# RWKV-7 recurrence without identity products, its first level on VectorE, head sums and spreads in two array groups

## The reference

```python
kk = heads(k * k_k)
kk = kk / jnp.maximum(jnp.sqrt(jnp.sum(kk * kk, axis=-1, keepdims=True)), 1e-12)
def step(S, inp):
    r_t, w_t, k_t, v_t, kk_t, a_t = inp
    sa = jnp.einsum('bhvk,bhk->bhv', S, -kk_t)
    S = (S * w_t[:, :, None, :] + sa[..., None] * (kk_t * a_t)[:, :, None, :]
         + v_t[..., None] * k_t[:, :, None, :])
    return S, jnp.einsum('bhvk,bhk->bhv', S, r_t)
# mean and variance of y over each head, then gn_w, gn_b, and
y = y + jnp.sum(r_h * k_h * r_k, axis=-1, keepdims=True) * v_h
```

## Time and profile before

| | |
|---|---|
| profiled execution, its own time | 3829.3 us |
| its span | 3827.5 us |
| mean granted TensorE clock | 0.912 |
| PE busy, whole span | 3199.8 us, 84% |
| DVE, ACT, POOL busy | 42%, 28%, 16% |
| first to last L1105 (start of a step on PE) | 1041.0 to 1969.0 us |

### The profile page before, as it was taken

One profiled execution on the slowest core, in us unless ns is written; L12 is line 12 of the kernel. 1 busy time (PEld: TensorE's weight loads), 2 busy tenths in 40 slices (PEclk: granted clock), 3 DMA queues, 4 the chain that ended last, 5 costly groups with the idle time before them and its releaser, 6 DMA issues. The chain is left out here.

```text
span 3827.5 us, 80050 instructions
## 1 busy us (share of the span) xinstructions
PE 3199.8 (84%) x35142; PEld 2529.9 (66%) x35142; DVE 1604.6 (42%) x2556; ACT 1069.8 (28%) x1930; POOL 613.2 (16%) x405
## 2 busy tenths in 40 slices
PE   3799999987588888888884984999899979992199
PEld 1687888852277777777773862888677877771077
DVE  4433333434355555555543115222277107774421
ACT  2222222212344444434342013110122115461110
POOL 0222222125221222122210000000000000342200
PEclk7899999999798999989896987999899989996599
DMA  4212222111521212222203331111122234233433
GB/s 147 77 59 80 72 69 77 58 44 77 175 69 47 74 49 72 58 64 59 62 25 116 115 126 55 39 33 34 32 66 72 73 105 138 75 96 124 131 99 110
DMA packets 287269, 301.64 MB, mean 79 GB/s; under 512 B 11807, under 2 KB 221855, under 8 KB 285296
## 3 DMA queue, kind: packets, MB, share of 16 engines
q1 hardware_dynamic: 255392, 217.64, 18.7%
q10 hardware_dynamic: 28512, 71.33, 4.8%
q0 software_dynamic: 3056, 8.05, 0.9%
HBM read 187.41 MB, written 114.25 MB: 79 GB/s over the span
## 5 line engine op out<-in xcount | busy, mean ns | idle before, releaser
L414 PE MATMUL pj_ps<-pj_x_hi,pj_w_hi 128*128 128x512 f32 x1024 | 402.1, 393 | 68.4 <-DVE pj_x_lo L369 60.1
L414 PE MATMUL pj_ps<-pj_x_lo,pj_w_hi 128*128 128x512 f32 x1024 | 400.8, 391 | 0.0
L414 PE MATMUL pj_ps<-pj_x_hi,pj_w_lo 128*128 128x512 f32 x1024 | 400.7, 391 | 0.0
L414 PEld LDWEIGHTS pj_ps<-pj_x_hi,pj_w_hi 128*128 128x128 f32 x1024 | 193.6, 189 | 112.4 <-issue 61.9
L348 POOL TENSOR_TENSOR pj_x<-h 128x512 f32<-128x512 f32 x128 | 168.0, 1313 | 575.4 <-DVE pj_x_lo L369 512.7
L369 DVE TENSOR_TENSOR pj_x_lo<-pj_x,pj_x_hi 128x512 fp32r<-128x512 f32 x128 | 89.2, 697 | 356.7 <-ACT pj_x_hi L424 356.7
L1483 PE MATMUL o_ps<-o_y_hi,o_w_hi 128*128 128x512 f32 x512 | 160.3, 395 | 85.2 <-DVE o_w_lo L1493 85.2
L414 PEld LDWEIGHTS pj_ps<-pj_x_lo,pj_w_hi 128*128 128x128 f32 x1024 | 193.8, 189 | 40.1
L414 PEld LDWEIGHTS pj_ps<-pj_x_hi,pj_w_lo 128*128 128x128 f32 x1024 | 193.6, 189 | 40.2
L958 DVE TENSOR_TENSOR rw_w<-rw_ps,rw_cst 128x512 f16<-128x512 f32 x160 | 105.1, 687 | 266.9 <-PE rw_ps L1123 266.9
L847 ACT CAST rw_x<-rw_ps 128x512 f16<-128x512 f32 x192 | 113.8, 592 | 290.8 <-PE rw_ps L1139 204.0
(11 more groups left out here) (250 smaller groups left out, 6616.3 us busy)
## 6 DMA issues: line engine op xcount, KB each, us to landing
proj<-pj_out ACTq DMA_DIRECT2D x128, 256.0 KB, 2.4
pj_w<-w_in SPq DMA_DIRECT2D x32, 512.0 KB, 4.1
proj<-lr_out ACTq DMA_DIRECT2D x32, 512.0 KB, 2.6
partial<-wa_ob SPq DMA_DIRECT2D x48, 264.0 KB, 2.1
mg_part<-partial SPq DMA_DIRECT2D x16, 792.0 KB, 4.5
wa_vt<-v_rows SPq DMA_DIRECT2D x43, 260.0 KB, 3.0
h<-xT SPq DMA_DIRECT2D x8, 1024.0 KB, 12.8
rw_k<-proj SPq DMA_DIRECT2D x16, 512.0 KB, 4.0
```

The source lines that it names most:

```text
L414: mm = pe.matmul(ps[i][:], wp, xp, start=k == 0 and m == 0, stop=k == KT - 1 and m == len(parts) - 1)
```

## The change

Six edits, all in the recurrence:

- The unit diagonal moves into the masks (`merge` minus the unit matrix) and into a second f16 copy of the matrix, `lt_less` (the matrix minus the unit), so that the merge products carry X themselves. L1130, L1147, L1148 and `first_level` go.
- Level 0 is done on DVE at the end of the step before: `less_unit` (4 instructions of 256 columns), `seeds` (2 of 512 for `y16`, 2 transposes in 32x32 blocks for `x16`). `first_masked` goes.
- `sums_by_head` writes even and odd pairs j to two groups of 32 columns, `spread` reads them from two groups of 32 rows, into two banks. `kss`, `kinv`, `glog`, `ginv` have 64 rows instead of 32.
- `turn`, `turn_centred` and the bonus work by halves g, with 64-row weights.
- `solve(f, 0)` and `m_from_values` are interleaved product by product. The keys' squares (ACT) and head sums (PE) move to the end of the step before.
- On DVE, `kmax` moves ahead of the masks, `kk` ahead of the last two decay sums, `kp` ahead of the fourth mask, and `ysum` behind `bt`. The residual's eviction multiplies by a mask.

```diff
-    put("merge", np.concatenate(merge, 1))
+    put("merge", np.concatenate([m - 1.0 * (sc == tc) for m in merge], 1))
@@ DVE
+            def less_unit(n, f, jh):
+                J = slice(4 * jh, 4 * jh + 4)
+                for g in range(2):
+                    n.need("a_sb", 2 * jh + g + 1)
+                    if f:
+                        f.need("e")
+                    n.did(dve.tensor_tensor(lt_less[:, g, J, :], mat_b[n.t % 2][:, g, J, 0:CHUNK],
+                                            const("unit", CHUNK).unsqueeze(1).to_broadcast([128, 4, CHUNK]),
+                                            ALU.subtract), "lt_less")
+            def seeds(n, f):
+                for g in range(2):
...
+                    n.did(dve.tensor_tensor(y16[:, g], lt_less[:, g], over_heads(seed16[:]), ALU.mult), "seed")
+                for g in range(2):
+                    n.need("seed", g + 1)
+                    n.did(dve.transpose(wide(x16, g), wide(y16, g)), "turned")
@@ PE
             def sums_by_head(src, b):
                 for j in range(KT):
-                    last = pe.matmul(PS[0:32, b, 0:128], sel(j), src[:, j, :], start=j == 0, stop=j == KT - 1)
+                    P = slice(32 * (j % 2), 32 * (j % 2) + 32)
+                    last = pe.matmul(PS[P, b, 0:128], sel(j), src[:, j, :], start=j < 2, stop=j >= KT - 2,
+                                     skip_group_check=True)
             def spread(weights, src, at):
-                for j in range(KT):
-                    last = pe.matmul(two(at)[:, j, :], weights(j), src[:], start=True, stop=True)
+                for i in range(KT // 2):
+                    for r in range(2):
+                        P = slice(32 * r, 32 * r + 32)
+                        last = pe.matmul(bank(at + r, 128)[:, i, :], weights(P, i), src[P, :], start=True, stop=True,
+                                         skip_group_check=True)
             def merges(f, l):
                 for g in range(2):
-                    f.need("w_sb", 2 * l + g + 1)
-                    pe.matmul(PS[:, XB[g], :], ident16[:], wide(x16, g), start=True, stop=False, skip_group_check=True)
+                    f.need("w_sb", 2 * (l - 1) + g + 1)
...
-            def turn(f, src, i):
-                for jh in range(2):
-                    for jj in range(4):
-                        last = pe.transpose(bank(6 + jh, 128)[:, jj, :], src[:, 4 * jh + jj, :], const("ident"))
+            def turn(f, src):
+                for j in range(KT):
+                    for g in range(2):
+                        last = pe.transpose(bank(6 + g, RW_N)[:, j, :], src[R, j, :], const("ident")[R, R])
+            def solve_and_m_from_values(f):
+                for j in range(KT):
+                    solve_one(f, 0, j, 0)
+                    m_one(f, 1, j, 1)
+                    m_one(f, 1, j, 0)
+                    last = solve_one(f, 0, j, 1)
...
+                    m_one(f, 0, j, 1)
+                    m_one(f, 0, j, 0)
```

More of the change, by code:

```diff
@@ L850, in tokens_of, with key_squares @@
             def tokens_of(f, i, dst):
-                f.need("trans", i + 1)
-                f.did(act.copy(dst[:, 4 * (i % 2):4 * (i % 2) + 4, :], bank(6 + i % 2, 128)), "tok")
+                for g in range(2):
+                    f.need("trans", 2 * i + g + 1)
+                    f.did(act.copy(dst[:, :, rows(g)], bank(6 + g, RW_N)), "tok")
+            def key_squares(t):
+                if t < TILES:
+                    at = Tile(act, S, RW_PER, t)
+                    at.need("kkr")
+                    if t >= 3:
+                        Tile(act, S, RW_PER, t - 3).need("var")
+                    at.did(act.activation(sq[:], kkr[:], ACT.Square), "ksq")
             def half_z(f, ci):
@@ L907, in step @@
                 if f:
-                    level(f, 3)
-                    for i in range(2):
-                        tokens_of(f, i, b_tok)
+                    tokens_of(f, 0, b_tok)
                 if n:
@@ L914, in step @@
                     level(f, 4)
-                    for i in range(2, 4):
-                        tokens_of(f, i, k_tok)
+                    tokens_of(f, 1, k_tok)
                 if n:
@@ L923, in step @@
                     level(f, 5)
[L924 to L925 removed]
+                    tokens_of(f, 2, v_tok[f.t % 2])
                     for g in range(2):
@@ L1045, in step @@
                     n.did(dve.tensor_tensor(kt[:], am[:], csum[:], ALU.mult), "kt")
+                if f:
+                    for g in range(2):
+                        f.need("e", g + 1)
+                        f.did(dve.tensor_tensor(w16[:, g], bank(XB[g], CHUNK), over_heads(const("lower", CHUNK)),
+                                                ALU.mult), "e_sb")
+                if n:
+                    n.need("b")
+                    n.did(dve.tensor_tensor(bt[:], bt[:], csum[:], ALU.mult), "bt")
                 if b:
@@ L1225, in z_from_state, with solve_one, m_one @@
                 f.did(last, "z")
+            def solve_one(f, ci, j, g):
+                R = chunk(ci)
+                return pe.matmul(bank(ZB[g], RW_N)[R, j, :], xt32[R, g, j, :], z_sb[R, g, j, :],
+                                 start=True, stop=True, skip_group_check=True)
+            def m_one(f, ci, j, g):
+                R = chunk(ci)
+                pe.matmul(bank(MB[ci], RW_N)[rows(g), j, :], k_tok[R, j, rows(g)], v_tok[f.t % 2][R, j, rows(g)],
+                          start=j == 0, stop=True, skip_group_check=True)
+            def solve_and_m_from_values(f):
+                f.need("z_sb0", 1)
+                f.need("z_sb1", 1)
+                f.need("yt_sb")
+                for j in range(KT):
+                    solve_one(f, 0, j, 0)
+                    m_one(f, 1, j, 1)
+                    m_one(f, 1, j, 0)
+                    last = solve_one(f, 0, j, 1)
+                    if j == KT - 1:
+                        f.did(last, "u")
+                    m_one(f, 0, j, 1)
+                    m_one(f, 0, j, 0)
             def solve(f, ci):
@@ L1229, in solve, with key_sums @@
                 f.need("z_sb1", ci + 1)
-                R = chunk(ci)
                 for j in range(KT):
                     for g in range(2):
-                        last = pe.matmul(bank(ZB[g], RW_N)[R, j, :], xt32[R, g, j, :], z_sb[R, g, j, :],
-                                         start=True, stop=True, skip_group_check=True)
+                        last = solve_one(f, ci, j, g)
                 f.did(last, "u")
-            def m_from_values(f):
-                for j in range(KT):
-                    for ci, g in ((0, 0), (1, 1), (0, 1), (1, 0)):
-                        R = chunk(ci)
-                        pe.matmul(bank(MB[ci], RW_N)[rows(g), j, :], k_tok[R, j, rows(g)],
-                                  v_tok[f.t % 2][R, j, rows(g)], start=j == 0, stop=True, skip_group_check=True)
+            def key_sums(t):
+                if t < TILES:
+                    at = Tile(pe, S, RW_PER, t)
+                    at.need("ksq")
+                    if t > 0:
+                        at.prev("a_sb", 6)
+                    at.did(sums_by_head(sq, 6), "ksum")
             def m_from_solved(f, ci):
@@ L1279, in step @@
                 if f:
-                    products(f, 1)
+                    merges(f, 1)
                 if b:
@@ L1296, in step @@
                 if b:
+                    y_from_state(b)
+                if f:
+                    products(f, 3)
+                    if n:
+                        n.need("kk")
+                    turn(f, bt)
+                    merges(f, 3)
+                if b:
                     b.need("ysq")
@@ L1325, in step @@
                         b.need("yn")
-                    for j in range(KT):
-                        last = pe.matmul(two(4)[:, j, :], rkbd[:, j, :], rk[:, j, :], start=True, stop=True)
-                    f.did(last, "bonus")
+                    bonus(f)
                     z_from_state(f, 0)
```

228 lines of the change are left out of this document (104 added, 124 removed).

## The result

The changed kernel took 3718.06 us (median of 4 runs, 3714.11 to 3726.58), the kernel before 3819.56 in the same comparison (4 runs, 3814.56 to 3828.93). The ratio is 0.9734, 95% interval 0.9707 to 0.9761: 101 us less. The forecast was 3697, range 3640 to 3760. In the profiled executions 3829.3 became 3720.72, 108.6 less.

A forecast was written before the change was run, and what follows sets the result against it. PE was taken to bound the kernel, 61.7 us a step; about 54 after, 7.7 saved fifteen times (116), plus 4 and 8, gives 128 off 3829.3: 3701 profiled, 3697 predicted. Range 3640 to 3760.

The forecast's parts named there:

- the 11.9: PE work removed per step at full clock: level 0 1.95, identity products 4.3, sums and spreads 3.8, turns and centring 1.9.
- Sums and spreads, 3.8: Two head sums and two spreads a step each halve if two groups run side by side: 3.8 us saved, bounds 0 and 3.8.
- The rival without overlap: Groups of 32 do not overlap and the turns do not shorten: 58 us a step, 3759 us; chance 12%.
- Merges, mixed group, bonus: PE per step: merges 0.54 us per half, interleaved solve and value products 2.9, bonus over two quarters 1.84.
- Identity products, 4.3: Ten identity products in the merges, 0.32 us each, 3.2, and four in the residual, 1.1, leave PE each step.
- The centring, 1.9 for turns and centring together: Two turns fall from 0.93 to 0.55 us each, the centring from 1.98 to 1.0; together 1.9 saved, bounds 0 and 2.
- `less_unit`, 0.4 each and 1.3 for the second pair: DVE at the step's end: 256-column operations about 0.4 us each; the second half's two, behind POOL's `lt_lo`, 1.3.
- The waits in the levels, 5.05: PE waits inside the levels grow to 5.05 us a step against about 1.5 before: 3.5 given back.
- The end of the step: From `z_from_state` on, PE's idle time becomes 7.15 us against 5.9: 1.3 given back.
- The low clock, 3.2: Low clock adds 3.2 us a step, against 3.7 before, partly on stretches in which PE waits anyhow.
- rival "slower": Granted clock falls as PE's busy share drops; 26 us of low clock a step lose the gain; chance 3%.
- The sum: 58 - 11.9 + 3.5 + 1.3 = 50.9 us a step at full clock, about 54 with the low clock; saved 7.7 a step.

The follow-up runs named there:

- serial order: Changed kernel with the same products reordered, all of one array group before the other's, in sums, spreads, turns, centring and bonus: 3794.72 us, ratio 0.9922.
- pair of edits: Changed kernel with the first half's solve ahead of all value products and `lt_less` taken from `lt_hi` in f16 ahead of the seeds: 3681.16 us, ratio 0.9646.
- small fill: Changed kernel with 272 more 64x64 products a step, read by nobody, put into PE's waits: 3778.92 us, ratio 0.9874.

## Why the prediction was right, and where its sizes were off

The mechanism was right: PE loses about 12 us of work a step (12.1 by the count, 11.9 forecast), a part comes back, and the period falls by 6 to 8 us. But the part that comes back is another one than forecast, and that the total fitted is partly luck. Luck is in the 11.9 too: centring and sums fell short by 1.4 together, and what made up for it is not shown. The forecast had 12.2 us of waits a step (5.05 + 7.15) and 3.2 of low clock; the count has 9.5 idle, gaps without a named cause included, and 7.9 added by the low clock. Waits grew by 1.3 us instead of 4.8, the price of the clock by 4.7 instead of falling. By its steps:

- **Sums and spreads, 3.8.** Measured 1.07 and 1.10 instead of the forecast 0.93 and 0.99: 3.3 for two of each. The serial order, in which they take 1.53 and 1.71, shows that the overlap is the cause of a little over half of it; the rest came with the split itself. The rival without overlap fell.
- **Merges, mixed group, bonus.** 0.53 per half, 3.0 and about 1.8, nearly as worked out. The bonus's two row halves write one bank at different partitions, and alternating they take 1.8 where one after the other they take 2.7 (1497.49 to 1500.17 in the serial kernel): they overlap, though not wholly, and the trace again disagrees with Gotcha 1: PSUM Pressure of the Trainium skill, "TensorEngine Tiling (Array Packing)", by which it would take about twice its 1.84.
- **Identity products, 4.3.** PE's time was right (3.2 forecast for the merges' ten, 3.7 by the count when they came back), but they are worth only 0.9 to 1.4 a step: the rest lies in gaps without a named cause and in a better clock.
- **The centring, 1.9 for turns and centring together.** This step failed in part. The turn was sized well (0.64 against 0.55). The centring was taken as half of a 128-column group, 1.0, and took 1.93 at full clock: the constant that it moves has 64 columns now, but the values are the weights, 128 columns of f32 as before, and such a pass costs about 60 ns side by side, twice the 31 of L1210, whose weights have 64. No row of before shows this shape in two groups. The bounds for turns and centring, 0 and 2, held the measured 0.6 + 0.05; the value taken stood near the wrong one.
- **`less_unit`, 0.4 each and 1.3 for the second pair.** It took 2.23 and 1.70 a pair: 0.41 for the one that runs without POOL, as forecast, and 1.89 and 1.37 for the one that starts during an operation of POOL. The forecast saw the collision with `lt_lo` and not the one with L815. This made the wait for `bv` 2.38 where 1.85 was forecast; the pair of edits showed that it, with the mixed group, was worth 2.2 us a step.
- **The waits in the levels, 5.05.** 0.73 and 0.54 ahead of level 4 (forecast 0.65 and 0.7), 1.06 ahead of kt's turn (1.35), 0.25 to 0.54 ahead of the centring (0.7), 0.66 and 0.29 in the residual (0.5 and 0.45), none ahead of levels 2 and 5 (0.4 and 0.3). The places were right, the sum was too large: 3.5 in this step and 2.9 on average (41 us from 1041 to 1850).
- **The end of the step.** The wait for the second half's state was 0.60, not 1.85, and there was none ahead of its solve in this step; `half_u` 1.06 (1.3), the next products 0.79 (0.95). With the 2.38 that is 4.8 instead of 7.15.
- **The low clock, 3.2.** This is the term that was furthest off. The line gives 3.6 us, but that is only how the step's length goes with the clock; the count gives 7.9 us of longer work. The clock, 0.85, lies outside the 0.88 to 0.94 that I named, and low time doubled from 8.5 to 16.7 us a step. The forecast put a part of the low stretches on waits; PE was busy in 94% of them. The rival "slower" named the right way for the clock. Its 26 us of low time are also a slip: 61.7 less 50.9, at 0.5 each, are 22.
- **The sum.** 50.9 at full clock against 52.4 by the line, 54 against 55.9 (7.7 against 5.9 saved a step). The centring (0.9) and the wait for `bv` (0.5) add up to the 1.5, but the sums (0.5) and the shorter waits above stand beside them, so this is no account of it. From 3701 for the profiled execution, 7 above the median, follow 3694 and not the 3697 of the forecast, a slip of 3 us. Nothing was saved ahead of the first tile: its first product of a level starts at 1041.0 in both kernels.

The period of 55.9 lies within the named 52 to 57.

## What to carry to other kernels

Work out a group's cost on TensorE from its weights too: the f32 group with a 128-column weight side took 1.93 us in two groups and 0.98 as twice as many products with 64 columns. Issue the groups in alternation: here that was worth more (77 us) than ten products less a step (13 us). When a wait has two causes, an edit that removes one shows little; test them together before calling either harmless. An operation that takes three times its usual time beside another engine costs what someone waits for it: the 2.23 of `less_unit` cost a wait. And look in the new trace whether a changed order has ended such a collision or only handed it to the next operation, as with am. Last, a low clock is read from how busy the engine is in it, not from its mean alone.

## What was not expected of the hardware

- PE stands still inside runs of small products, for up to about 2 us at a time and up to 3.6 in the small fill, in gaps that no engine causes: 20 us from 1041 to 1850 in the changed kernel at 1408 instructions a step (8 with the same instructions in the longer steps of the serial order), 37 and 31 with 32 more (but 22 in a third), 89 with 336 more, 2 when ten wide products stand among them. That PE runs out of instructions there would fit, and is only argued. The Trainium skill, "Runtime: NRT & Kernel Launch", Instruction fetch mechanics, says that the fetch runs ahead and its cost is mostly hidden; if it is the cause, it was not hidden here.
- A two-input operation of DVE with both inputs in SBUF that starts while POOL runs one is not slowed by a factor: it ends at a fixed time behind POOL's. `less_unit` takes 0.41 alone; started 0.22 or 0.55 us into L815 it takes 1.95 or 1.62, and ends 0.28 behind it both times, as it does behind `lt_lo`. am takes 1.2 alone and ends 1.08 behind POOL's product for b, 3.30 in all. POOL's own 1.91 and 2.37 stay. It also goes the other way: where DVE's product started 0.2 us ahead, POOL's product for b took 3.23, 0.87 more. An operation that reads PSUM and SBUF is not held: the pair of L999 keeps its 1.29 beside POOL.
- What a low microsecond adds to the step is not what it adds to PE's work: 0.22 against 0.47 after the change, 0.54 (plus or minus 0.12) against 0.38 before.
